# Sums over a head's features: four groups of 32 array columns in place of one of 16, stored as 128 rows

## What is computed

```
kk = heads(k * k_k)
kk = kk / jnp.maximum(jnp.sqrt(jnp.sum(kk * kk, axis=-1, keepdims=True)), 1e-12)
...
mean = jnp.mean(y, axis=-1, keepdims=True)
var = jnp.mean(jnp.square(y - mean), axis=-1, keepdims=True)
y = ((y - mean) * lax.rsqrt(var + RWKV_LN_EPS)).reshape(bsz, seq, W) * ln_w + ln_b
bonus = jnp.sum(r * k * r_k, axis=-1, keepdims=True) * v
```

## Time and profile before

| | us |
|---|---|
| median of 3 runs | 2795.69 (2793.8 to 2796.46) |
| the profiled execution | 2797.11 |
| its span in the trace | 2795.9 |
| TensorE busy | 2765.7 (99%) |
| VectorE busy | 1734.5 (62%) |
| ScalarE busy | 1346.7 (48%) |
| mean granted TensorE clock | 0.999 |

### The profile page before, as it was taken

The page is one execution under the profiler, slowest core; times in us unless marked ns, Lnnn a source line. Parts: engine busy times, 40 slices in busy tenths (PEclk is TensorE's granted clock), DMA queues, the critical chain, the costliest instruction groups (busy, mean ns, idle before and its releaser), DMA issues.

```text
span 2795.9 us, 40955 instructions
## 1 busy us (share of the span) xinstructions
PE 2765.7 (99%) x17183; PEld 2364.6 (85%) x17183; DVE 1734.5 (62%) x2045; ACT 1346.7 (48%) x1741; POOL 43.3 (2%) x71
## 2 busy tenths in 40 slices
PE   8999989999999999999999999999999999999998
PEld 7888888888888888888888888888888888888887
DVE  5787668654655655555555566556766656665675
ACT  6745434544554444434444545554554444443444
POOL 2000000000000000000000100000000000000001
PEclk9999999999999999999999999999999999999999
DMA  7565317566455656666666555555556555555554
GB/s 235 161 201 182 103 56 244 175 196 196 153 176 184 185 192 194 188 192 189 196 186 194 181 187 189 166 169 177 174 173 196 188 191 194 181 196 196 190 187 136
DMA packets 395317, 506.69 MB, mean 181 GB/s; under 512 B 11441, under 2 KB 287422, under 8 KB 394366
## 3 DMA queue, kind: packets, MB, share of 16 engines
q1 hardware_dynamic: 380925, 488.26, 54.2%
q10 hardware_dynamic: 14208, 15.81, 1.9%
HBM read 501.87 MB, written 2.17 MB: 180 GB/s over the span
## 4 chain that ended last, share of the span: by engine, by line
PE 94%; DVE 2%; ACT 1%; SPq 1%; issue 1%; DMA 0%; ACTq 0%; DVEq 0%
PE PS L697 38%; PE PS L702 33%; PE PS L706 16%; PE PS L952 3%; DVE wlo L2189 1%; PE PS L745 1%; PE PS L1166 0%; PE PS L1186 0%; PE PS L728 0%; PE PS L874 0%; PE PS L1243 0%; SPq L364 0%; ACT whi L1499 0%; PE PS L1135 0%; DMA raw<-in_w_in 0%
## 5 line engine op out<-in xcount | busy, mean ns | idle before, releaser
L2189 DVE TENSOR_TENSOR wlo<-raw,whi 128x1024 fp32r<-128x1024 f32 x922 | 1128.5, 1229 | 783.3 <-ACT whi L1499 779.6
L1499 ACT ACTIVATE whi<-raw 128x1024 fp32r<-128x1024 f32 x922 | 969.7, 1056 | 930.5 <-PE PS L706 455.0
L702 PE MATMUL PS<-XX,whi 128*128 128x512 f32 (+1 forms) x3856 | 1216.0, 397 | 0.8 <-DVE wlo L2189 0.6
L706 PEld LDWEIGHTS PS<-XX,wlo 128*128 128x128 f32 (+1 forms) x3856 | 724.5, 188 | 171.3
L706 PE MATMUL PS<-XX,wlo 128*128 128x256 f32 (+1 forms) x3856 | 759.9, 278 | 0.0
L697 PE MATMUL PS<-whi,act 128*128 128x512 f32 x2208 | 593.1, 390 | 0.0
L702 PEld LDWEIGHTS PS<-XX,whi 128*128 128x128 f32 (+1 forms) x3856 | 589.1, 189 | 3.8 <-issue 2.4
L697 PEld LDWEIGHTS PS<-whi,act 128*128 128x128 f32 x2208 | 411.7, 188 | 84.0
L697 PE MATMUL PS<-wlo,act 128*128 128x512 f32 x1104 | 340.0, 389 | 0.0
L697 PE MATMUL PS<-whi,XX 128*128 128x512 f32 x1024 | 279.2, 394 | 4.0 <-DVE wlo L2189 2.6
L697 PEld LDWEIGHTS PS<-wlo,act 128*128 128x128 f32 x1104 | 207.2, 188 | 43.5
(11 more groups left out here) (418 smaller groups left out, 1438.3 us busy)
## 6 DMA issues: line engine op xcount, KB each, us to landing
raw<-in_ffn_w SPq DMA_DIRECT2D x128, 1024.0 KB, 5.5
raw<-in_w_in SPq DMA_DIRECT2D x103, 1024.0 KB, 5.0
raw<-in_w_ffn_gate SPq DMA_DIRECT2D x44, 1024.0 KB, 4.9
raw<-in_w_ffn_up SPq DMA_DIRECT2D x44, 1024.0 KB, 4.9
raw<-in_w_ffn_down SPq DMA_DIRECT2D x44, 1024.0 KB, 5.2
raw<-in_w_out SPq DMA_DIRECT2D x32, 1024.0 KB, 5.2
raw<-in_xattn_wk SPq DMA_DIRECT2D x16, 1024.0 KB, 5.5
raw<-in_xattn_wv SPq DMA_DIRECT2D x16, 1024.0 KB, 5.1
```

What stands on the lines that cost most here:

```text
L702: T.matmul(ps[0:wd, f, :], whi[:, o:o + wd], b.x[:, kk, :], start=first, stop=False, skip_group_check=True)
L706: mm = T.matmul(ps[0:wd, f, 0:SEQ], wlo[:, o:o + wd], b.x[:, kk, 0:SEQ], start=False, stop=last, skip_group_check=True)
L1499: S.activation(k.whi[:, h % 4, 0:b.size], k.raw[:, t % 4, u * b.size:(u + 1) * b.size], ACT.Copy).then_inc(k.w_hi, 1)
L2189: V.tensor_tensor(k.wlo[:, h % 4, 0:b.size], k.raw[:, h // 2 % 4, u * b.size:(u + 1) * b.size], k.whi[:, h % 4, 0:b.size].bitcast(F32), AL ...
```

## The change

`head_sum` places the matmul of block f = 2q + m at array columns 32q to 32q + 31, and its result in PSUM partitions 32q to 32q + 31. The four groups q are visited in turn, first with m = 0, then with m = 1, which adds into the same partitions. Head h = 2f + e then stands in row 16f + e of 128; the other rows are zero. One selector of 48 columns serves all blocks, read at two offsets; `sel_rk` holds 8 blocks of 32 columns and 16 columns of zeros. `hs` and `bs` take all 128 partitions, the root, the reciprocal, the copy and the stores cover them, and the DRAM tensors have 128 rows. The loads pick rows 16f + e. GpSimd makes one more memset, and smaller selections.

```
--- before.py
+++ after.py
@@ -161,7 +161,7 @@
         self.m_in = sb("m_in", [P, P])
         self.m_lk, self.m_ll = sb("m_lk", [P, 4, RC]), sb("m_ll", [P, 2, RC])
         self.m_ar, self.m_kr = self.m_lk[:, 0:2, :], self.m_lk[:, 2:4, :]
-        self.sel = sb("sel", [P, RP, 16])
+        self.sel = sb("sel", [P, 48])
         self.idc, self.rst = sb("ident_compact", [P, RC]), sb("rst", [P, SEQ])
 
         self.head_mean = sb("head_mean", [P, P])
@@ -173,7 +173,7 @@
         self.mul = sb("mu_lora", [P, 4])
 
         self.rest = sb("one_less", [P, RP + 24])
-        self.sel_rk = sb("sel_r_k", [P, RP, 16])
+        self.sel_rk = sb("sel_r_k", [P, 32 * RP + 16])
         self.dtb, self.alog, self.dsk, self.fxb = (sb(n, [P, m]) for n, m in (
             ("dt_bias", 16), ("a_log", 16), ("d_skip", 16), ("fox_bias", 8)))
         own_at = nc.sbuf_base
@@ -244,7 +244,7 @@
         self.Aexp = v(24944, 16)
 
         self.HP = slice(96, 112)
-        self.hs, self.bs = v(23568, SEQ)[self.HP, :], v(23824, SEQ)[self.HP, :]
+        self.hs, self.bs = v(23568, SEQ), v(23824, SEQ)
         self.eend, self.DTf = v(25472, RP, NRC), v(25504, SEQ)
 
         self.xdt, self.y = v(2048, NT, SSD_W), v(20480, NT, SSD_W)
@@ -270,8 +270,8 @@
 
 
         self.norm_rows = v(0, RP, SEQ)
-        self.norms_out = [self.nc.dram_tensor(f"norms{n}", (RWKV_H, SEQ), F32).ap() for n in range(2)]
-        self.bonus, self.bonus_out = over(3, 0, RP, SEQ), self.nc.dram_tensor("bonus", (RWKV_H, SEQ), F32).ap()
+        self.norms_out = [self.nc.dram_tensor(f"norms{n}", (P, SEQ), F32).ap() for n in range(2)]
+        self.bonus, self.bonus_out = over(3, 0, RP, SEQ), self.nc.dram_tensor("bonus", (P, SEQ), F32).ap()
         self.mem_by_token = [v(7168, D), v(21504, D)]
         self.PX = pairs(v(18432, RP, 3 * RC), 3), pairs(over(3, 0, RP, 3 * RC), 3)
         self.KT = v(19968, RP, RC), over(3, 1536, RP, RC)
@@ -867,12 +867,14 @@
         yield
 
 
-def head_sum(k, src, bank, n=SEQ, sel=None):
-
-    sel = k.sel if sel is None else sel
-    for f in range(RP):
-        mm = k.nc.tensor.matmul(k.PS[k.HP, bank, 0:n], sel[:, f, :], src[:, f, :], start=f == 0,
-                                stop=f == RP - 1)
+def head_sum(k, src, bank, n=SEQ, sel_rk=None):
+
+    for m in range(2):
+        for q in range(4):
+            f, at = 2 * q + m, 16 * (1 - m)
+            sel = k.sel[:, at:at + 32] if sel_rk is None else sel_rk[:, 32 * f + at:32 * f + at + 32]
+            mm = k.nc.tensor.matmul(k.PS[32 * q:32 * q + 32, bank, 0:n], sel, src[:, f, :], start=m == 0, stop=m == 1,
+                                    tile_position=(0, 32 * q), skip_group_check=True)
     return mm
 
 
@@ -909,7 +911,7 @@
         yield
     T.wait_ge(*rp.DVE("rk"))
     T.wait_ge(k.rest_made, 2)
-    head_sum(k, k.t1, 4, sel=k.sel_rk).then_inc(rp.pe, 1)
+    head_sum(k, k.t1, 4, sel_rk=k.sel_rk).then_inc(rp.pe, 1)
     for _ in range(7):
         yield
 
@@ -1828,7 +1830,7 @@
 
     S = k.nc.scalar
     S.wait_ge(k.norm_stored[n], 16)
-    src = k.norms_out[min(n, 1)][:, tok].rearrange("(f e) t -> e f t", e=2)
+    src = k.norms_out[min(n, 1)][:, tok].rearrange("(f a) t -> a f t", a=16)
     for e in range(2):
         S.dma_start(dst[64 * e:64 * e + 64], src[e].unsqueeze(0).to_broadcast([64, RP, tok.stop - tok.start])
                     ).then_inc(k.norm_there[n], 16)
@@ -1855,7 +1857,7 @@
     ins.then_inc(rp.act, 1)
     yield
     S.wait_ge(*rp.PE("n2"))
-    S.activation(k.hs, k.PS[k.HP, 4, 0:SEQ], ACT.Sqrt).then_inc(rp.act, 1)
+    S.activation(k.hs, k.PS[:, 4, 0:SEQ], ACT.Sqrt).then_inc(rp.act, 1)
     yield
     yield
     S.wait_ge(*rp.DVE("hs"))
@@ -2117,7 +2119,7 @@
     S.wait_ge(*k.ry.PE("y", NRC - 1))
     S.wait_ge(k.bonus_stored, 16)
     for e in range(2):
-        S.dma_start(k.bonus[64 * e:64 * e + 64, :, :], k.bonus_out.rearrange("(f e) t -> e f t", e=2)[e].unsqueeze(0)
+        S.dma_start(k.bonus[64 * e:64 * e + 64, :, :], k.bonus_out.rearrange("(f a) t -> a f t", a=16)[e].unsqueeze(0)
                     .to_broadcast([64, RP, SEQ])).then_inc(k.bonus_there, 16)
     S.dma_start(k.g2, i["rwkv_g2"][0].rearrange("(a p) n -> p a n", p=P)).then_inc(k.g2_w, 16)
     mem_tile_act(k, 0)
@@ -2594,7 +2596,7 @@
     yield
     yield
     V.wait_ge(*rp.PE("bon"))
-    V.tensor_copy(bs, PS[k.HP, 4, 0:SEQ]).then_inc(rp.dve, 1)
+    V.tensor_copy(bs, PS[:, 4, 0:SEQ]).then_inc(rp.dve, 1)
     for _ in range(5):
         yield
 
@@ -2686,7 +2688,7 @@
 def post_dve(k, h):
     V, tok = k.nc.vector, slice(P * h, P * h + P)
     ro, col, hs, v4, pt1 = k.ro[h], k.col, k.hs[:, tok], k.quarters(4 + 2 * h), k.pt1[:, :, tok]
-    R, VV, sums = k.RKV[:, 0:8, tok], k.RKV[:, 16:24, tok], k.PS[k.HP, 4 + 2 * h, 0:P]
+    R, VV, sums = k.RKV[:, 0:8, tok], k.RKV[:, 16:24, tok], k.PS[:, 4 + 2 * h, 0:P]
     yield
     V.wait_ge(*ro.PE("mb"))
     V.tensor_tensor(R, R, v4, ALU.subtract).then_inc(ro.dve, 1)
@@ -2943,7 +2945,8 @@
     V.wait_ge(*k.par.ACT("col0"))
     opened_split(s, raw_feed_dve(k, 0, k.col["norm_mix_g"]), lambda q: None, first_scale_dve, rest_dve(k))
     V.wait_ge(k.const_sem, k.const_total)
-    V.tensor_tensor(k.sel_rk[:, :, :], k.sel[:, :, :], k.bc(k.col["rwkv_r_k"], 16), ALU.mult).then_inc(k.rest_made, 1)
+    V.tensor_tensor(k.sel_rk[:, 0:32 * RP].rearrange("p (f h) -> p f h", h=32), k.rep(k.sel[:, 0:32], RP),
+                    k.bc(k.col["rwkv_r_k"], 32), ALU.mult).then_inc(k.rest_made, 1)
     prepared(s, lora_dve(k), prep_dve(k))
     V.wait_ge(*k.rp.DVE("end"))
     ssd_steps = ssd_dve(k)
@@ -3029,6 +3032,7 @@
     for t, v in ((k.ones, 1.0), (k.triu, 1.0), (k.negu, 0.0), (k.sel, 1.0),
                  (k.m_in, 1.0), (k.head_mean, 1.0 / 64), (k.idc, 0.0), (k.rst, 1.0), (k.m_kr, 1.0), (k.m_ll, -1.0)):
         made(G.memset(t[:, :] if len(t.shape) == 2 else t[:, :, :], v))
+    made(G.memset(k.sel_rk[:, 32 * RP:], 0.0))
     made(G.memset(k.m_ar[:, 0, :], 1.0))
     made(G.memset(k.m_ar[:, 1, :], -1.0))
     up = lambda t, fill, base=0: select(t[:, :], one, base, -1, ge, fill)
@@ -3053,8 +3057,8 @@
         same_block(k.m_ar[r, 1, :], 16)
         same_block(k.m_ll[r, 0, :], 16)
     made(G.tensor_tensor(k.m_ll[:, 1, :], k.m_ll[:, 1, :], k.m_ll[:, 0, :], ALU.subtract))
-    select(k.sel[:, :, :], [[128, RP], [-64, 16]], 0, 1, ge, 0.0)
-    select(k.sel[:, :, :], [[-128, RP], [64, 16]], 63, -1, ge, 0.0)
+    select(k.sel[:, :], [[-64, 48]], 1024, 1, ge, 0.0)
+    select(k.sel[:, :], [[64, 48]], 63 - 1024, -1, ge, 0.0)
     select(k.rst[:, :].rearrange("p (c e) -> p c e", e=RC), [[0, NRC], [1, RC]], -1, 0, ge, 0.0)
     k.const_total = done
 
```

## The result

The changed kernel takes 2809.28 us (median of 4 runs, 2806.52 to 2811.31) against 2795.33 us for the kernel before (4 runs): a ratio of 1.0048, 95% interval 1.0036 to 1.006. It is slower by 14 us, where 2 us less were forecast. The profiled execution is the quickest of its four, 2806.52 us with a span of 2805.3; the profiled one of before has 2795.9. So the two traces show 9.4 us of the 14.

The account below looks back on a forecast made before the run. TensorE, busy for 99% of the span, was taken as the bound, with VectorE full in stretches. Gains of 2.34 + 0.30 less 0.36 and 0.20 for stores gave 2.08 us: 2793.6 us from 2795.69, range 2790.5 to 2797.0.

Parts of the forecast that it names:

- the one on the stores: Stores of norms and bonus: 128 rows for 16 cost 0.36 us at the first, 0.20 at the later ones, bonus 0.
- the store becomes the bound: Rival: the first norms' store, with ScalarE waiting, lands as late as the load's 6.6 us; 2796.7 us, chance 0.08.
- three signs of being wrong: Calls keep their lengths, the second call starts 2 us earlier, or the first store takes over 5 us.
- the 2.34 us kept: Second call (164.32): starts unchanged, ends 2.70 us earlier; 2.34 us travel on before the next weights wait for their low part.
- priced at 0 with the bonus: Bonus store, waited for only when ScalarE copies the states 100 us later: 0, or 0.4 us if uncovered.
- The store's term: First norms' store: 7 more packets per DMA engine at 51 ns each, 0.36 us longer than 3.2 us, off the gain.
- four tiles at once: Head sums: four 32-column matmuls overlap fully, so a long call falls from 3.56 to 0.86 us, a short one 1.79 to 0.45.
- The half rate: Rival in the head sums: only two matmuls at once, 1.5 us gained, 2794.2 us; with no overlap 2796.3; chance 0.10.
- the emptying of the array: Rival in the head sums: every tile change drains the array, a long call takes 6.2 us; 2806.9 us, chance 0.03.
- The third is hidden in the wait for the fourth: Third call (428.58): ends 1.34 us earlier, but the fourth waits for VectorE's squares anyway, so nothing is gained.
- No link of this chain waits for the first call: VectorE's chain to the second call is independent of the first call (121.35), whose 2.70 us saving therefore gives 0.
- The fourth call's 0.30 us: Fourth call (430.72): frees TensorE 1.34 us earlier, but the half at 464.34 can move only 0.30 us behind VectorE.

Follow-up runs that it names:

- The other four kernels with old sums: The kernel before with only the distance between a load's eight rows changed, to 4, 8, 16 or 17 KB: 2798.4, 2815.1, 2819.0 and 2795.3 us.
- the padded kernel: The changed kernel with each DRAM row 64 bytes longer, so a load's eight rows lie 17 KB apart: 2790.64 us, ratio 0.9983 against the kernel before.
- the sum made four times: The changed kernel with rows 64 bytes longer and its second sum (the bonus) made four times over: 2793.36 us, ratio 0.9993 against the kernel before.
- the long sum: The changed kernel with rows 64 bytes longer and its first sum (of kk * kk) made four times over: 2790.84 us, ratio 0.9985 against the kernel before.
- the old kernel at 17 KB: The kernel before, old sums and 16 stored rows, with a load's eight rows 17 KB apart: 2795.3 us, ratio 1.0001.

## Why the prediction was wrong

**The step that failed** is the one on the stores. It priced the 128 rows on their way out and let the loads back stand: "The rows of the sums are stored as 128 in place of 16", and 6.6 us of the broadcast load were only a bound for the store. The front of this document says that the loads pick rows 16f + e: eight rows of 1 KB, 16 KB apart for 2 KB. Their duration is the term that was missing: 12.2 us for 6.6 in the first norms, 12.3 for 7.6 in the bonus, 12.6 for 9.7 in the later norms. The same distance alone makes the old kernel 24 us slower, and its removal makes the changed one 18.6 us faster. The rival "the store becomes the bound" had the right place (ScalarE and VectorE without slack behind the norms) and the wrong transfer. None of the three signs of being wrong that the prediction names came up: the calls got shorter, the second started later, the first store was quick. None of them looked at a load.

**Where it enters.** VectorE's wait of 4.47 us for the norms makes the second call 2.6 us late (3.55 when counted from the first call), as much as that call saves: of the 2.34 us kept nothing is left. The larger part I had priced at 0 with the bonus, "waited for only when ScalarE copies the states", and meant its store. Its loads share ScalarE's queue with what stands behind them, and TensorE pays between 416 and 473. In both places together, about 5.9 us of what it pays are matmuls at 1.2 GHz, the estimate above.

**The store's term, with the wrong sign.** 0.36 us more were expected; it came 1.5 us sooner, 1.7 us. In the kernel before, 30 of the 32 packets that ScalarE's queue has around the store start in 135.7 to 136.1 us, then comes an instruction load of 16 KB, and two more start after 137.0. The rows are the queue in 135.7 to 136.1, the instruction load in 136.1 to 137.15, and the queue in 137.0 to 137.3:

```profile
q10 hardware_dynamic: 30, 0.02, 14.8%
q8 instruction: 1, 0.02, 5.7%
q10 hardware_dynamic: 2, 0.00, 3.1%
```

The other four kernels with old sums have such a late packet too, 0.7 to 1.0 us behind the rest, and take 2.8 to 3.1 us for the store. In the changed kernel the instruction load near it starts at 132.2 and is over when the store is issued at 133.82. That the load holds up one row of the store is a reading; the trace doesn't name the DMA engine of a packet, and nothing was tried.

**Right:** four tiles at once. A long call went from 3.56 to 1.00 us; 0.86 and the gaps were forecast. The half rate (1.78 us) and the emptying of the array (6.2 us), both rivals, are out. The sixteen instructions of a long call, on four places, start within 0.7 us. With that the statement of the Trainium skill (TensorEngine Tiling, section Tiling Modes) agrees that a change of tile alone does not drain TensorE. The second call is on the path: in the padded kernel the half behind it comes at 171.95, with the sum made four times at 174.49, 2.54 us of 2.6 later, and 2.34 us kept were forecast. The third is hidden in the wait for the fourth. The first is hidden in the time, but not wholly in the trace. "No link of this chain waits for the first call" is not quite right: with the long sum ScalarE waits 1.51 us for TensorE before 130.87, and VectorE 0.33 us for ScalarE before 142.65.

**The fourth call's 0.30 us was too small.** In the padded kernel its gain stays: the half after it comes at 426.56 and, with the same distance as in the earlier trace rows, the later one at 458.33. TensorE in that kernel:

```profile
425.98 0.65 PE L876 MATMUL PS<-slab,sel 128*32 128x128 f32 x16 [1.51 <-DVE slab L2696]
426.56 1.19 PE L697 MATMUL PS<-whi,XX 128*128 128x512 f32 x4
...
458.33 1.07 PE L697 MATMUL PS<-whi,XX 128*128 128x512 f32 x4
```

31.77 us lie between the two, 31.77 before: no wait is added. I had taken VectorE's chain after 455.48 as fixed, but it begins with a DMA, the norms' loads, and these fell from 9.7 to 6.5 us. The narrow tiles are worth 4 to 5 us with that and the quicker store (0.9983 against 1.0001 of the old kernel at 17 KB, 4.6 us by the medians), where 2.64 were forecast for the sums alone.

**Open:** the traces show 9.4 of the 14 us. Two of the four runs of the changed kernel are 4 to 5 us above the profiled one, and the trace is of another; whether they stood longer at 1.2 GHz is not known.

## What to carry to other kernels

When a change alters how rows are laid out in DRAM, price the loads that read them and not only the store: the bytes were the same and the loads took up to twice as long. Where a load reads a few rows many times and they would lie a multiple of 8 KB apart, lengthen them a little; 64 bytes a row, 1 KB between the rows of a load, were enough here, and less was not tried. Count a long wait of TensorE at more than its length, since the matmuls behind it ran at half the clock here. And a queue's slow DMA costs the ones behind it, and the engine that issues them.

## What the runs showed of the hardware that was not expected

Loads that read eight rows of 1 KB over and over, into 64 partitions each, took 67 to 73 ns a packet at 2, 4, 17 and 20 KB between the rows, 106 at 8 KB, 123 at 24 KB and 134 to 158 at 16 KB. The Trainium skill (DMA: Bandwidth & Descriptors, section Latency and other measured facts) has a like loss in copies between HBM tensors: 207 GB/s at a row pitch of 512 KiB, 164 at 2 MiB, 103 at 4 and 8 MiB; at 4 MiB it was cured by 4 KiB more and not by 192 B. Here the loss is small at 4 KB (3.3 us of the kernel), large at 8 (20 us) and 16 KB (24 us), and 1 KB more in the stride ends it. A store of 128 rows of 1 KB landed in 1.7 us; of 16 rows in 2.8 to 3.2.
